# Expert jobs in strict turn of 128 and 64 rows, a ring of 28 weight slots, four split buffers

## The reference

```
logits = h @ router_w;  top_val, top_idx = top_k(logits, 2);  top_w = softmax(top_val)
y = sum over e of  gate_e * ((silu(h @ wg[e]) * (h @ wu[e])) @ wd[e])
```

## Time and profile before

| | us |
|---|---|
| median of three runs | 1511.85 |
| the profiled execution | 1511.59 |
| its span, from the first to the last instruction | 1509.8 |
| PE busy | 1448.8 (96%) |
| DVE busy | 980.3 (65%) |
| ACT busy | 835.9 (55%) |
| DMA, mean over the span | 309 GB/s |

### The profile page before, as it was taken

How to read it: one execution, slowest core, us unless ns; L and a number is a source line. 1 busy time by engine, 2 the same in 40 slices (tenths; PEclk the granted TensorE clock), 3 DMA queues, 4 the chain that set the end, 5 groups by cost and what they waited for, 6 DMA issues and landing times.

```text
span 1509.8 us, 20323 instructions
## 1 busy us (share of the span) xinstructions
PE 1448.8 (96%) x6996; PEld 1073.4 (71%) x6996; DVE 980.3 (65%) x1306; ACT 835.9 (55%) x1084; POOL 36.7 (2%) x48
## 2 busy tenths in 40 slices
PE   9999999999999999999999988999887999888998
PEld 8887888888888777788888423888323888325787
DVE  5878665445587866998998202998104988105997
ACT  6657564344665756777877102776002876004885
POOL 2000010000000000000000000000000000000000
PEclk9999999999999999999999999999999999999999
DMA  9544475555455548899999999999999999999995
GB/s 359 189 141 168 151 270 193 178 185 167 140 167 168 168 167 293 307 398 367 367 388 372 337 404 411 405 399 411 407 410 409 405 401 411 402 409 410 405 409 203
DMA packets 207507, 466.13 MB, mean 309 GB/s; under 512 B 13288, under 2 KB 15600, under 8 KB 207408
## 3 DMA queue, kind: packets, MB, share of 16 engines
q1 hardware_dynamic: 203376, 452.50, 80.5%
q0 software_dynamic: 3856, 12.25, 2.2%
q10 hardware_dynamic: 176, 0.07, 0.0%
HBM read 457.68 MB, written 7.09 MB: 308 GB/s over the span
## 4 chain that ended last, share of the span: by engine, by line
PE 84%; DMA 5%; DVE 5%; ACT 3%; issue 2%; SPq 1%; ACTq 0%; DVEq 0%
PE pA L627 57%; PE pB L627 8%; PE pA L1183 8%; PE pA L1193 4%; DMA raw<-expert_w_up_dram 2%; PE pB L651 2%; DVE w_lo L1630 2%; SPq L470 1%; ACT w_hi L1265 1%; DMA raw<-expert_w_gate_dram 1%; PE pA L651 1%; DMA more<-expert_w_up_dram 1%; DMA more<-expert_w_gate_dram 1%; ACT ex_act L1594 1%; PE pB L1202 1%
## 5 line engine op out<-in xcount | busy, mean ns | idle before, releaser
L1630 DVE TENSOR_TENSOR w_lo<-raw,w_hi 128x1024 fp32r<-128x1024 f32 x426 | 501.3, 1219 | 111.4 <-ACT w_hi L1265 108.4
L1265 ACT ACTIVATE w_hi<-raw 128x1024 fp32r<-128x1024 f32 x426 | 432.0, 1057 | 123.1 <-PE pA L627 48.3
L627 PE MATMUL pA<-w_hi,hT_hi 128*128 128x512 f32 x848 | 337.7, 398 | 11.8 <-DVE w_lo L1630 11.7
L627 PE MATMUL pA<-w_hi,hT_lo 128*128 128x512 f32 x848 | 331.7, 391 | 0.0
L627 PE MATMUL pA<-w_lo,hT_hi 128*128 128x512 f32 x848 | 331.6, 391 | 0.0
L627 PEld LDWEIGHTS pA<-w_hi,hT_hi 128*128 128x128 f32 x848 | 159.9, 189 | 50.6 <-DVE w_lo L1630 16.3
L627 PEld LDWEIGHTS pA<-w_hi,hT_lo 128*128 128x128 f32 x848 | 159.9, 189 | 34.2
L627 PEld LDWEIGHTS pA<-w_lo,hT_hi 128*128 128x128 f32 x848 | 160.1, 189 | 31.4
L2193 DVE TENSOR_TENSOR ex_act<-pA,ex_act 64x512 f32<-64x512 f32 x21 | 14.6, 694 | 246.4 <-ACT ex_act L1594 246.4
L1630 DVE TENSOR_TENSOR w_lo<-more,w_hi 128x1024 fp32r<-128x1024 f32 x140 | 165.7, 1219 | 11.6 <-ACT w_hi L1265 9.4
L1265 ACT ACTIVATE w_hi<-more 128x1024 fp32r<-128x1024 f32 x140 | 147.0, 1060 | 39.2 <-PE pA L627 31.0
(11 more groups left out here) (386 smaller groups left out, 1782.6 us busy)
## 6 DMA issues: line engine op xcount, KB each, us to landing
raw<-expert_w_down_dram SPq DMA_DIRECT2D x131, 512.0 KB, 11.0
raw<-expert_w_gate_dram SPq DMA_DIRECT2D x129, 512.0 KB, 11.2
raw<-expert_w_up_dram SPq DMA_DIRECT2D x124, 512.0 KB, 10.9
more<-expert_w_up_dram SPq DMA_DIRECT2D x87, 512.0 KB, 11.0
raw<-w_in_dram SPq DMA_DIRECT2D x43, 1024.0 KB, 5.0
more<-expert_w_gate_dram SPq DMA_DIRECT2D x74, 512.0 KB, 11.1
more<-expert_w_down_dram SPq DMA_DIRECT2D x63, 512.0 KB, 11.3
toep<-expert_w_down_dram SPq DMA_DIRECT2D x30, 512.0 KB, 11.5
```

The lines of the kernel that those rows point to most:

```text
L627: ins = mm(o, r if swap else l, l if swap else r, start=first and n == 0, stop=True, skip_group_check=True)
L1265: f(w_hi[:, m % PARTS, :], raw_slot(m), ACT.Copy).then_inc(s["w_hi_done"], 1)
L1630: tt(w_lo[:, m % PARTS, :], raw_slot(m), w_hi[:, m % PARTS, :].bitcast(F32), ALU.subtract).then_inc(s["w_lo_done"], 1)
```

## The change

- The jobs alternate strictly: 0, 2, 4, 6 are wide, 1, 3, 5, 7 narrow. So there are four narrow jobs in place of three, for the four of experts 1 to 7 with the fewest rows, and the last job is narrow. The loop's rounds are (narrow, wide), and a last narrow job follows.
- The ring has 28 slots. Three of the seven new ones are the pad behind `more`, and four (`last_slots`) are space of the fifth and sixth split buffers, which the mixers and the dense layer still use (`early_hi`, `early_lo`) but the experts no longer do. The pad lies over the rows of normalised x, so it is free once these are stored and gathered. `last_slots` is free once the last piece before the experts is used.
- In the experts there are four split buffers in place of six, and `after` splits 3 pieces ahead in place of 4. The first four pieces are still split before job 0.
- On DVE in a narrow job, `turned(c - 1)` comes ahead of the multiplication of chunk c.
- At the end of a narrow job, ACT scales the result rows, not DVE, and DVE splits the next job's first pieces without waiting for the end of the narrow job on PE.
- The last job, narrow now, keeps its result on chip: ACT and DVE scale 64 rows each of `B2`, PE adds them to the sum with four plain float32 matmuls, and the output follows in four DMAs.

```
-RING = 21
-PARTS = 6
-AHEAD = 4
+RING = 28
+PARTS, EXPERT_PARTS = 6, 4
+AHEAD, EXPERT_AHEAD = 4, 3
-WIDE_JOBS = NE - PAIRS
+WIDE_JOBS = NE - PAIRS - 1
 def is_narrow(j):
-    return j > 0 and j % 2 == 0
+    return j % 2 == 1
...
+        last_slots = eb("last_slots", [P, 2 * (PARTS - EXPERT_PARTS), PIECE])
-        more = eb("more", [P, RING - 2 * RAW - 2, PIECE])
-        eb("behind_more", [P, 3 * PIECE])
+        more = eb("more", [P, 7, PIECE])
+        behind_more = eb("behind_more", [P, 3, PIECE])
...
# SP, slot_free
+                elif owner < 0 and r < BEHIND0:
+                    sp.wait_ge(s["obT_lo_done"], 2 * NL)
+                elif owner < 0 and r < LAST0:
+                    sp.wait_ge(s["normed_stored"], 32)
+                    sp.wait_ge(s["gather_psum"], 2)
                 elif owner < 0:
-                    sp.wait_ge(s["obT_lo_done"], 2 * NL)
+                    sp.wait_ge(s["w_used"], EX0)
...
# PE, the end
+            def scatter(j):
+                pe.wait_ge(s["y_rows_done"], 2 * j + 2)
                 for a in range(A):
+                    for half in range(2):
+                        rows = slice(NARROW * half, NARROW * (half + 1))
+                        mm(sum_bank(a, half), spread[rows, a, :].bitcast(F32), y_rows[rows, 0:512],
+                           start=(half == 0), stop=True, skip_group_check=True).then_inc(s["scatter_psum"], 1)
...
# PE, ACT and DVE
             with pe.Fori(0, rounds) as i:
-                job(2 * i + 1, i + 1)
-                narrow_job(i, 2 * i + 2)
-            job(2 * rounds + 1, rounds + 1, last=True)
+                narrow_job(i, 2 * i + 1)
+                job(2 * i + 2, i + 1)
+            narrow_job(rounds, 2 * rounds + 1, last=True)
...
# ACT, split_to
+                    parts = EXPERT_PARTS if m >= first_of[0] else PARTS
                     if m >= PARTS:
-                        eng.wait_ge(s["w_used"], piece_count(m - PARTS, w))
+                        eng.wait_ge(s["w_used"], piece_count(m - parts, w))
...
# DVE, narrow_job
                 for c in range(NCX):
+                    if c:
+                        turned(c - 1)
                     eng.wait_ge(s["n_silu_done"], NCX * i + c + 1)
                     tt(ex_act[NARROW:, c % 2], (B0, B1)[c % 2][NARROW:, :], ex_act[NARROW:, c % 2], ALU.mult)\
                         .then_inc(s["n_act_done"], 1)
-                    if c:
-                        turned(c - 1)
...
# DVE, place_jobs
-                link(ts(places[:, 0:NE], ranks, 2.0, 1.0, ALU.mult, ALU.add))
-                link(stt(places[:, 0:NE], narrow, float(1 - 2 * WIDE_JOBS + 2), places[:, 0:NE], ALU.mult, ALU.add))
+                link(ts(places[:, 0:NE], ranks, 2.0, 2.0, ALU.mult, ALU.add))
+                link(stt(places[:, 0:NE], narrow, float(1 - 2 * WIDE_JOBS), places[:, 0:NE], ALU.mult, ALU.add))
```

More of the change, by code:

```diff
@@ L1063, in gather_narrow, with first_slots, spread_rows @@
                         ins.then_inc(s["gather_psum"], 1)
[L1065 to L1083, removed]
+            def first_slots():
+                pe.wait_ge(s["plan_ready"], 1)
+                for a in range(A):
+                    ins = slot_row(a)
+                ins.then_inc(s["slot_psum"], 1)
+            def spread_rows():
+                for a in range(A):
+                    ins = turn(B7[:, P * a:P * (a + 1)], pick[:, a, :].bitcast(F32), a == 0)
                 ins.then_inc(s["slot_psum"], 1)
@@ L1097, in next_rows, with job @@
                 ins.then_inc(s["from_psum"], 1)
-            def scatter_first():
-                pe.wait_ge(s["y_lo_done"], 1)
+            def scatter(j):
+                pe.wait_ge(s["y_rows_done"], 2 * j + 2)
                 for a in range(A):
[L1103 to L1123, removed]
+                    for half in range(2):
+                        rows = slice(NARROW * half, NARROW * (half + 1))
+                        mm(sum_bank(a, half), spread[rows, a, :].bitcast(F32), y_rows[rows, 0:512],
+                           start=(half == 0), stop=True, skip_group_check=True).then_inc(s["scatter_psum"], 1)
+            def job(j, w, first=False):
                 for kind, c, at, n in expert_order:
@@ L1226, in narrow_job @@
                         downs(c - 1)
-                    if c == 2:
+                    if c == 2 and last:
+                        spread_rows()
+                    if c == 2 and not last:
                         next_rows(j + 1)
-                    if c == 5:
+                    if c == 5 and not last:
                         gather_rows(j + 1, (B3, B6))
                 downs(NCX - 1)
+                if last:
+                    pe.wait_ge(s["part_added"], 2 * A)
+                    for a in range(A):
+                        mm(sum_bank(a, 1), ident, x[:, a, 512:], start=True, stop=True, skip_group_check=True)
+                    scatter(j)
             keep_busy(3)
@@ L2003, in _ @@
             counts, places = plan[:, 0:NE], plan[:, 8:8 + JOBS]
[L2004 removed]
+            ranks, narrow, far = [plan[:, c:c + NE] for c in (24, 32, 40)]
             nc.vector.tensor_copy(counts, B7[:, 16:24])
@@ L2194, in narrow_job @@
                         .then_inc(s["n_act_done"], 1)
-                    if c:
-                        turned(c - 1)
-                    if c == 1:
+                    if c == 1 and not last:
                         eng.wait_ge(s["rows_stored"], 16 * j)
```

258 lines of the change are left out of this document (121 added, 137 removed).

## The result

The changed kernel takes 1477.52 us in the median (four runs: 1475.26, 1475.27, 1479.77 and 1480.35; the end of this document has what is known of the gap between them), the kernel before 1511.82 in the same series: ratio 0.9774, 95% interval 0.9751 to 0.9796, so 34.3 us less. The profiled execution took 1475.26 at a span of 1473.4, so 10.6 us less than the 1484.0 of the sum.

A forecast was written before the change was run, and what follows sets the result against it. PE was taken to set the pace in wide jobs 0 and 1, DMA from 900 us. Span 1474.3 + 1.5 + 8.2 = 1484.0 us; with 1.8 and 0.3 more, 1486 us, range 1478 to 1498.

The forecast's parts named there:

- the sum: Whole span after the change: last bytes at 1474.3, split buffers 1.5, what follows the bytes 8.2, together 1484.0 us.
- DVE's turn: Narrow jobs: DVE's new order removes PE's waits for `act_narrow`, 11.9 us a job, worth nothing more in the middle.
- four split buffers, 3 ahead: Wide jobs: fewer split buffers cost 1.5 us in job 0, with -1 and +7 as ends; later jobs cover it.
- seven slots more: Ring: seven more pieces issued when the first narrow job begins, 7 x 1.324 = 9.3 us earlier last bytes.
- slots spread wider: Rival: DMA loses 4% of its rate, taking all 26 us; chance 0.02, 0.02 more for slower by such a cause.
- DMA sets the pace from the first narrow job on: From 723.6 us DMA is the limit at 1.324 us a piece, so last bytes come at 1474.3 us.
- Order: Experts: the first narrow job begins where job 1 did, which brings the last bytes 8.9 us earlier.
- The end: After the last bytes: 8.2 us, ends 7.1 and 9.5, in place of 17.3; 9.1 us saved.
- The ring full at the start of job 1: End of job 0: the ring can be full at 723.6 us, 91 pieces needing 120.5 of 123 us.
- no more DMA in job 0: Rival: DMA gives no more in job 0, first bytes 9 us late, 1490 to 1495 us; chance 0.12.
- PE's clock: Rival: gaps in jobs 3, 5 and 7 take PE's clock down for good, 1665 us, slower; chance 0.03.
- SP's waits "nearly gone": Sign in job 0: SP's waits nearly gone and DMA at 400 GB/s from about 605 us.

The follow-up runs named there:

- e2: The kernel before with only the unused pad tensor `to_line2` cut from 120 to 104 floats (64 bytes less): 1498.96 us, ratio 0.9917.
- e6: The changed kernel with 21 slots and all six split buffers, 4 ahead: 1482.59 us, ratio 0.9807.
- e4: The changed kernel with 21 ring slots in place of 28: 1484.36 us, ratio 0.983.
- e1: The changed kernel run once more, unchanged: 1475.77 us, ratio 0.9766.
- e3: The changed kernel with the unused pad tensor `to_line2` back at 120 floats: 1490.0 us, ratio 0.9854.
- e7: The changed kernel without the product of `w_lo` with the high part of `hT` or `ex` in jobs 2, 4 and 6: 1480.44 us, ratio 0.9782.
- e9: The changed kernel with the ten slots of `more` and `behind_more` moved by 64 bytes, operands not moved: 1481.61 us.
- e13: The changed kernel with the ten slots of `more` and `behind_more` moved by 128 bytes, operands not moved: 1480.93 us.
- e5: The kernel before with only DVE's new order in narrow jobs: 1511.7 us, ratio 0.9999.
- e14: The changed kernel with the ten slots of `more` and `behind_more` moved by 256 bytes, operands not moved: 1475.53 us.
- e11: The changed kernel with `last_slots` ahead of `behind_more` in the ring: 1475.27 us, ratio 0.9772.
- e15: The changed kernel with the ten slots of `more` and `behind_more` moved by 256 bytes and the experts' operands by 64: 1476.19 us.
- e10: The changed kernel with the ten slots of `more` and `behind_more` moved by 128 bytes and the experts' operands by 64: 1481.72 us.

## Why the prediction was wrong in size, and which of its steps held

From the medians 1511.8, 1499.0 (e2), 1482.6 (e6), 1484.4 (e4) and 1475.8 (e1) each part has a price:

| part | forecast | measured | from |
|---|---|---|---|
| order of jobs, DVE's turn and the end | -18.0 | -16.4 | e2 to e6 |
| four split buffers, 3 ahead | +1.5 | +1.8 | e6 to e4 |
| seven slots more | -9.3 | -8.6 | e4 to e1 |
| the pad | not seen | -12.8 | before to e2 |
| all | -25.8 | -36.0 | before to e1 |

The first series has 34.3 us in place of 36.0, since two of its four runs fell near 1480.

- **What failed: the sum took the start of the first narrow job (723.6 + 1.5 = 725.1 us) and the pace (1.324 us a piece) from the kernel before, and had no term for the pad, which moves both.** Measured, that job starts at 719.03 us, 6.1 earlier; from there to the last bytes are 745.1 us where 750.7 were forecast, 5.6 less; the end is 1.1 longer than the 8.2 of the sum. Together that is the 10.6 us by which the span lies below 1484.0. Both early steps move with the pad's line alone (e2, e3).
- **What the pad's line is worth in the changed kernel.** Without it, e3 says, the time would be 1490.0: above the 1486 forecast, inside the range. The 4 us between are DMA's pace again: there 14 of 28 slots are off the place, before it was 7 of 21, and 1.3409 - 1.3313 over 560 pieces is 5.4 us. That is the "slots spread wider" of the last rival, at a fifth of the 26 us that it would have had to take.
- **DMA sets the pace from the first narrow job on: right.** PE relieved in jobs 2, 4 and 6 gave nothing (e7), DMA slowed by slots out of place cost 5 to 6 us (e9, e13). A smaller fault is the split of 648.8 us into 1.324 a piece and 9.3 of start-up: by the landings the pace before was 1.3313, so 483 x 1.3313 = 643.0 and 5.8 of start-up. The pace is what the shorter pad lowered, to 1.3234, and 560 x 1.3234 + 5.8 = 746.9.
- **Order: right.** In the profiles of e2 and e6 the last bytes land at 1479.81 and 1470.98, 8.8 us apart; 8.9 was forecast.
- **The end: 9.3 us in place of 8.2.** What lies behind the last bytes fell from 17.1 to 9.26, so 7.8 saved where 9.1 were forecast. The identity matmuls of L1233 stand behind the last piece on PE and hold the scatter until 1467.13, though `y_rows` was ready at 1465.50 + 0.76 = 1466.26. I had left them out of the sum. The other misses nearly cancel: the four matmuls take 2.0 us in place of 2.8, and from the last add's end (1469.84) to the span's end it is 3.6 in place of 2.8.
- **DVE's turn: nothing, as forecast**, shown by e5 in the kernel before.
- **The ring full at the start of job 1: right**, and sooner than needed. The rival "no more DMA in job 0" is refuted by 403 GB/s.
- **Split buffers: right in size**, 1.7 to 1.8 us for 1.5 (e4, e6). PE waited 1.8 us in job 0 for `w_lo`.
- **PE's clock: the rival is refuted.** The granted clock was 1.00 (2.4 GHz) from 960 to 1000 us with PE busy 36.77 of 40 us and from 1400 to 1440 us with 31.70 of 40. After an idle stretch of 3.5 us at the start of job 3 it was 0.86 from 930 to 950 us, so part of it at 1.2 GHz, and then 1.00 again. Over 880 to 1440 us it was 0.98. By the rule of the Trainium skill named with that rival ("TensorE: Matmul & The Clock Gate", section "What's actually happening") it would have come true only if the short gaps counted as idle, and in these rows they didn't.
- **SP's waits "nearly gone": wrong**, they are 74.8 us, because I took a queue's wait for idleness of what it feeds.

## What to carry to other kernels

A diff that resizes or adds a tensor, an unused one too, moves all that is behind it: before costing such a change, list which operands change their place against their partners, and price it. In a stage bound by DMA let the slots begin at multiples of 256 bytes, as all 28 do in e1, and keep a matmul's two operands in step. An experiment that undoes only the pad costs one line and would have come first, had I asked of each line of the diff what it does to the addresses.

## What the runs showed of the hardware

- **A transfer's place in SBUF.** A piece of 128 partitions x 4096 bytes takes 0.031 to 0.035 us longer (2.3 to 2.6% of 1.323) when its slot begins 64 or 128 bytes beyond a multiple of 256, and nothing longer when it is moved by 256. With all slots in place the rate is 410 GB/s, with 10 of 28 off 407, with 14 off 405.
- **A matmul's two operands.** 128x512 with a stationary operand 64 bytes out of step with the moving one takes 394 ns in the groups in place of 389, and starts 233 ns after the one before in place of 227. With both moved by 64 bytes it is 227 ns again, and with the moving one alone moved 229.7 (e3). Other distances weren't tried.
- **A lull of DMA.** In some executions the rate falls below 400 GB/s for 50 to 100 us, near 1100 us in both profiles that caught it (e7, e14), and the end comes 3 to 7 us later. Here the same 55 us of the changed kernel and of e7:

```profile
1080.00:1135.00 55.00, 54.70 (x257) 45.03 (x256) 50.25 (x48) 42.89 (x45) 0.00 (x0) 1.00 1.04 411
```

```profile
1080.00:1135.00 55.00, 45.87 (x170) 28.47 (x170) 50.05 (x47) 42.04 (x45) 0.00 (x0) 0.97 1.04 367
```

The DMA share is 1.04 in both, so the engines were occupied but moved less. Two of the first four runs of the changed kernel, one of five in e1, one of four in e4, three of four in e7, one of four in e11, two of five in e14 and one of five in e15 have times that fit it. None of the 17 runs with slots off their place (e3, e9, e10, e13) has; whether that is chance isn't shown. What causes the lull stays open; no run was made on it.
